# Pairing the value products of the third attention on TensorE, with a third pair of buffers for the turned probabilities

## The chip, the cores and the metric

The kernel runs on one core of one Trainium2 chip. The metric is the time of one execution on the device in microseconds (us), from three runs each. Beside these runs there is one profiled execution, from which all rows below are taken. It lasted 2522.84 us, and its span from the first to the last instruction is 2521.0 us.

## The reference, cut to what matters

Two transformer blocks follow each other on 512 tokens of width 1024. The first block has two layers with a differential attention. The second block has one layer with two attentions: a latent attention (MLA) and a sparse attention (NSA). The change touches only the last of these, which the code calls attention number 3 (`which > DEPTH`, with `DEPTH = 2`); the words "third attention" count kinds: differential, latent, sparse.

For eight heads of 64 columns in two key groups it computes three results, weighs each with a gate per token and head, and adds them:

```
p_c = softmax(where(valid_c, q kc^T * scale, NEG)) * valid_c    # 31 compressed keys
o_s = softmax(mask(q ks^T * scale)) vs                          # selected blocks, causal
o_w = softmax(mask(q kw^T * scale)) vw                          # window of 256, causal
o   = g0 * (p_c vc) + g1 * o_s + g2 * o_w
```

With 512 tokens all eight blocks of 64 keys are selected, so `o_s` is a plain causal attention over up to 512 keys.

## The kernel before, in words

Each engine runs its own straight program, written out in order, and waits on semaphores. Nothing is planned at run time: the order of the instructions in the code is the order on each engine.

**The steps.** `nsa_steps` (L304) lists 36 steps, numbered 0 to 35. Step 0 is a compressed step (kind "cmp") for the heads t and t + 4 of the first tile. Each of four tiles then has eight ordinary steps: for each block b of 128 queries one over the selected keys, which are (b + 1) times 128 wide, and one over the window, at most 384 wide. Behind block 1 of each tile but the last stands the compressed step of the next tile. So the compressed steps are 0, 5, 14 and 23. The tiles open at steps 1, 10, 19 and 28 and close at 9, 18, 27 and 35. The widest steps, with 512 keys, are 8, 17, 26 and 34. A step holds two heads, one on each half of the partitions.

**What a step asks of each engine.** TensorE computes the scores of both heads (`scores`, L2184, or L2179 in a compressed step). VectorE adds the masks and takes the maxima (`maxes`, L1319 and L1321; L1304 to L1307 if compressed). ScalarE takes the exponentials (L661). VectorE scales the first head's probabilities (`weigh`, L1355 to L1363, or L1335 to L1339 for both heads of a compressed step), ScalarE those of the second head (L684). TensorE transposes them into PSUM (`turn`, L2205, or L2201). ScalarE copies the result into SBUF (`copy`, L676). TensorE multiplies values by it and adds into one PSUM bank (`apply`, L2225; `apply` of a step that opens a tile also multiplies the compressed part, L2219). A compressed step has no `apply` of its own.

**TensorE's order.** `attention` (L2166) ends with a loop over s from 0 to 35; this text calls one pass "iteration s". In this attention an iteration holds `scores(s + 2)`, then `turn(s, 0)` and `turn(s, 1)`, then one or two pieces (three 512-column matmuls each, L2241) of another product, the gate projection `gate_nsa1`, and then `apply(s - 1)`. After the loop comes `apply(35)`.

**Who waits for whom.** `turn(s, 0)` waits for VectorE's `weigh(s)` and for the copy of `turn(s - 1, 0)`, whose PSUM bank it reuses. `apply` waits for the step's copy. The apply that opens a new tile also waits until the last tile's result has left its bank: ScalarE writes `y_hi` (L697) and VectorE `y_lo` (L1145). The loops of ScalarE (L693) and VectorE (L1379) have the same steps. VectorE does `maxes(s + 2)`, then `weigh(s + 1)` in its iteration s. ScalarE does `copy(s)`, the second half of `weigh(s + 1)`, then the exponentials of step s + 2. Both also split the next block of gate weights into a high part (ScalarE, L570) and a low part (VectorE, L1139), one at a time in this loop.

**Buffers.** The copied, turned probabilities lie in two pairs of buffers, the pair s % 2 for step s (`turned_to`, L389). `copy(s)` waits on the count `pv_done` that TensorE raises at the end of each `apply`, up to that of step s - 2.

Of the kernel before, what the change touches and what calls it, by code (L numbers as in the profile page):

```python
# [7 lines left out]
P = 128  # L8
# [3 lines left out]
DEPTH = 2  # L12
# [83 lines left out]
def program(nc, weights, ada, c_row_d, vecs_d, consts_d, x_t, p_t, pool_w, cmp_w1, cmp_w2, positions, out):  # L96
# [7 lines left out]
    with ctx:  # L104
        def sb(name, shape, dt=F32):
            return ctx.enter_context(nc.sbuf_tensor(name, shape, dt))
# [30 lines left out]
        pT = [sb(f"pT{i}", [P, S]) for i in range(2)]  # L137
        T = [sb(f"T{i}", [P, S]) for i in range(4)]
        qx = sb("qx", [P, 4, S])
# [34 lines left out]
        def sem(name):  # L174
            if name not in sems:
                sems[name] = ctx.enter_context(nc.semaphore(name))
            return sems[name]
# [73 lines left out]
        def evacuated(g, off4=0):  # L251
            return bank_free(g), TURN[g] + 1 + off4
# [47 lines left out]
        def turned_cmp(t, j):  # L300

            return (T[j] if t % 2 == 0 else qx[:, j, :])[0:CMP_W, :]
# [41 lines left out]
        def applied(which, s):  # L344

            done = [x for a in ATTENTION[:which] for x in a] + ATTENTION[which][:max(0, s + 1)]
            return sum(x["kind"] != "cmp" for x in done)
# [31 lines left out]
        def probs(which, m):  # L379

            return pads[:, m % 4, 0:S]

        def score_bank(m):
            return ps[2 + m % 4]
# [1 line left out]
        def both_scores(s):  # L386
            return psum[:, 2 + 2 * (s % 2):4 + 2 * (s % 2), :]

        def turned_to(s, j, diff):  # L389
            return pT[s % 2] if diff else (pT[0], pT[1], T[2], T[3])[2 * (s % 2) + j]  # L390

        def turns(which, s):

# [4 lines left out]
        def turn_bank(which, s, j):  # L398
            return ps[6] if which < DEPTH else ps[(6, 1)[(turns(which, s) + j) % 2]]
# [159 lines left out]
        def _(act):  # L559
            c = Counts()  # L560

            def split(n, g, off2=0, off4=0):

                if n >= NU:
                    return
                act.wait_ge(*loaded(n, off2))
                if n >= 2:
                    act.wait_ge(*tile_done(g - 1, off4))
                w = slice(0, width(n))
                act.activation(w_hi[n % 2][:, w], raw[n % 2][:, w], ACT.Copy).then_inc(sem("hi_made"), 1)  # L570
# [70 lines left out]
            def attention(which, between=None):  # L641
                steps = ATTENTION[which]
                diff = steps[0]["kind"] == "diff"
                along, plan = ALONG.get(which), pieces(which)
                n0, g0, _, tpu = ST[along[0]] if along else (0, 0, 0, 0)

                def exps(s):
                    x = steps[s]
                    for j in range(2):
                        exp(s, j, x)  # L650

                def exp(s, j, x):
                    m = 2 * s + j
                    if j == 0:
                        act.wait_ge(*c.next("max_made"))
                    if x["kind"] == "cmp":
                        act.activation(probs(which, m)[:, 0:P], score_bank(m)[:, 0:P], ACT.Exp)\
                            .then_inc(sem("exp_done"), 1)
                        return
                    k = m % 4  # L660
                    act.activation(probs(which, m)[:, 0:x["w"]], score_bank(m)[:, 0:x["w"]], ACT.Exp,  # L661
                                   bias=small[:, k:k + 1], scale=1.0,
                                   accum_out=small[:, 4 + k:5 + k]).then_inc(sem("exp_done"), 1)

                def copy(s, j, x):

                    act.wait_ge(*c.next("pT_in_psum"))
                    if applied(which, s - 2) > 0:

                        act.wait_ge(sem("pv_done"), applied(which, s - 2))  # L670
                    bk = turn_bank(which, s, j)
                    if x["kind"] == "cmp":
                        dst, src = turned_cmp(x["tile"], j), bk[0:CMP_W, :]
                    else:
                        dst, src = turned_to(s, j, diff)[:, 0:x["w"]], bk[:, 0:x["w"]]
                    act.activation(dst, src, ACT.Copy).then_inc(sem("pT_made"), 1)  # L676

                def weigh(s):

                    if "gate" not in steps[s]:  # L680
                        return
                    p = probs(which, 2 * s + 1)[:, 0:steps[s]["w"]]
                    act.wait_ge(*c.next("scale_made"))
                    act.activation(p, p, ACT.Copy, scale=small[:, 14 + s % 2:15 + s % 2])\  # L684
                        .then_inc(sem("second_weighed"), 1)

                exps(0)
                if between:
                    between(0)
                exps(1)  # L690
                if between:
                    between(1)
                for s in range(len(steps) + 2):  # L693
                    if s >= 2 and steps[s - 2]["closes"] and not diff:

                        act.wait_ge(sem("pv_done"), applied(which, s - 2))
                        act.activation(y_hi[:, steps[s - 2]["tile"], :], ps[7][:, :], ACT.Copy)\  # L697
                            .then_inc(sem("xhi_made"), 1)
                    if s < len(steps):
                        for j in range(1 if diff else 2):  # L700
                            copy(s, j, steps[s])
                        if s + 1 < len(steps):
                            weigh(s + 1)
                        if s + 2 < len(steps):
                            exps(s + 2)
                        for u, j, k in plan[s]:
                            if j == k == 0:
                                split(n0 + u + 1, g0 + u * tpu)
                            if k == KT - 1 and not diff:
                                to_gate(along[1] + tpu * u + j, g0 + tpu * u + j, 0, 0)  # L710
                    if diff and 1 <= s <= len(steps):
                        for u, j, k in plan[s - 1]:
                            if k == KT - 1:
                                to_gate_times(tpu * u + j, g0 + tpu * u + j)
# [1281 lines left out]
        def _(pe):  # L1996
# [169 lines left out]
            def attention(which, between=None):  # L2166
                steps, m0 = ATTENTION[which], MC[which]
                diff = steps[0]["kind"] == "diff"
# [39 lines left out]
                def apply(s):  # L2208
                    x = steps[s]
                    if x["kind"] == "cmp":  # L2210
                        return
                    pe.wait_ge(sem("pT_made"), TURNS[which] + turns(which, s + 1))
                    if diff and s == 0:
                        pe.wait_ge(*evacuated(ST[f"v{which}"][1] + 3))
                    if x["opens"] and any(y["closes"] for y in steps[:s]):
                        pe.wait_ge(*c.next("o_made" if diff else "x_made"))
                    for compressed in x.get("cmp", []):
                        pe.wait_ge(sem("vc_made"), 1)
                        pe.matmul(*compressed, start=True, stop=False)  # L2219
                    n = len(x["values"][0])  # L2220
                    for i in range(n):
                        for j in range(len(x["values"])):
                            v, p = x["values"][j][i], turned_to(s, j, diff)[:, i * P:(i + 1) * P]
                            a, b = (p, v) if diff else (v, p)
                            ins = pe.matmul(x["out"][j], a, b, start=x["first"] and i == 0,  # L2225
                                            stop=x["last"] and i == n - 1)
                    ins.then_inc(sem("pv_done"), 1)
# [22 lines left out]
                scores(1)  # L2250
                if between:
                    between(1)
                ahead = which > DEPTH
                for s in range(len(steps)):
                    if ahead and s + 2 < len(steps):
                        scores(s + 2)
                    for j in range(1 if diff else 2):
                        turn(s, j)
                    if not ahead and s + 2 < len(steps):
                        scores(s + 2)  # L2260
                    for at in plan[s]:
                        piece(*at)
                    if s >= 1:
                        apply(s - 1)
                apply(len(steps) - 1)

            def lam_sums():
                pe.wait_ge(sem("lam_terms"), 1)
# [139 lines left out]
            for k in range(KT):  # L2408
                w = weight(n, 56 * k, 56 * k + 56)
# [47 lines left out]
            for u in range(3):  # L2457
                ready(n + u)
                for i, t in enumerate((3, 2, 0, 1) if u == 0 else range(QB)):
# [4 lines left out]
                    for k in range(6):  # L2464
                        a, w = (f_hi[:, 2 + k, at], f_lo[:, 2 + k, at]), weight(n + u, 256 * k, 256 * k + 256)
# [292 lines left out]
```

## Time and profile before

| what | us |
|---|---|
| median of three runs | 2524.85 (2523.75 to 2526.11) |
| the profiled execution | 2522.84 |
| its span | 2521.0 |
| TensorE matmuls busy in the span | 2501.9 (99%) |
| VectorE busy | 1395.2 (55%) |
| ScalarE busy | 943.7 (37%) |
| the third attention, first loop scores to the next stage | 1970.84 to 2090.23 of the span |

A row of the time line has the start, the duration, the engine and line, the operation, the tile written and the tiles read, the shape and the number of instructions merged into the row. In brackets stands idle time of the engine before it and what ended it. PE is TensorE's matmuls, PEld its weight loads, DVE is VectorE and ACT is ScalarE. Matmuls are pipelined and their durations overlap, so the time that a group takes is read from its start to the start of the next group.

### The profile page before, as it was taken

The page shows a single profiled execution, that of the slowest core. Times are in us where ns is not written, and L with a number is a line of the kernel's source. Part 1 is how long each engine was busy: PE and PEld are TensorE (multiplying, and loading weights), DVE is VectorE, ACT ScalarE, POOL GpSimd, SP SyncE. Part 2 cuts the span into 40 slices and gives each one's busy share as a digit, 9 for nine tenths or more (in the row PEclk, how much of TensorE's full clock was granted, in tenths as well). Part 3 has the DMA queues.
Part 4 walks back from the last instruction along what each step waited for, and adds up shares of the span by engine and source line. Part 5 has one row for each costly group of instructions (what it writes and reads, how often), then busy time and mean ns, then how long its engine had stood idle before and what let it go on. Part 6 is the DMA issues. An engine that isn't in the chain of part 4 may idle for free.

```text
span 2521.0 us, 30069 instructions
## 1 busy us (share of the span) xinstructions
PE 2501.9 (99%) x11841; PEld 2023.9 (80%) x11841; DVE 1395.2 (55%) x1962; ACT 943.7 (37%) x1379; POOL 60.4 (2%) x77
## 2 busy tenths in 40 slices
PE   9999999999999999999999999999999999999999
PEld 7788888888888877888888888888777658888887
DVE  6556366645556655555663444566654676733433
ACT  5432334322334444223442232445544574422222
POOL 6000000000000000000001000000000001000000
PEclk9999999999999999999999999999999999999999
DMA  4222223444443311222343333222222111222222
GB/s 164 67 84 96 88 101 104 150 147 150 150 136 115 104 68 69 99 101 84 109 139 126 134 115 133 95 91 101 101 93 75 51 34 67 101 100 100 94 90 100
DMA packets 38629, 260.04 MB, mean 103 GB/s; under 512 B 4417, under 2 KB 4673, under 8 KB 8049
## 3 DMA queue, kind: packets, MB, share of 16 engines
q1 hardware_dynamic: 32976, 226.92, 26.2%
q10 hardware_dynamic: 5296, 30.20, 3.4%
q8 instruction: 83, 1.36, 0.2%
q0 software_dynamic: 240, 1.28, 0.2%
q14 instruction: 34, 0.27, 0.0%
HBM read 256.29 MB, written 2.10 MB: 102 GB/s over the span
## 4 chain that ended last, share of the span: by engine, by line
PE 94%; DVE 4%; ACT 1%; issue 1%; DMA 0%; SPq 0%; DVEq 0%; ACTq 0%
PE ps L2010 65%; PE ps L2037 9%; PE ps L2241 6%; PE ps L2063 5%; PE ps L2184 2%; PE ps L2225 2%; PE ps L2205 1%; PE ps L2467 1%; DVE w_lo L1139 1%; PE ps L2483 1%; PE ps L2163 0%; DVE a_lo L1263 0%; PE ps L2523 0%; PE ps L2329 0%; DVE T L1258 0%
## 5 line engine op out<-in xcount | busy, mean ns | idle before, releaser
L1139 DVE TENSOR_TENSOR w_lo<-raw,w_hi 128x2048 fp32r<-128x2048 f32 x208 | 477.5, 2295 | 325.1 <-ACT w_hi L570 275.3
L2010 PE MATMUL ps<-a_hi,w_hi 128*128 128x512 f32 x1408 | 550.4, 391 | 0.5 <-DVE w_lo L1139 0.3
L2010 PE MATMUL ps<-a_hi,w_lo 128*128 128x512 f32 x1408 | 547.9, 389 | 0.0
L2010 PE MATMUL ps<-a_lo,w_hi 128*128 128x512 f32 x1408 | 547.8, 389 | 0.0
L570 ACT ACTIVATE w_hi<-raw 128x2048 fp32r<-128x2048 f32 x198 | 376.4, 1901 | 404.0 <-PE ps L2010 338.2
L2010 PEld LDWEIGHTS ps<-a_hi,w_hi 128*128 128x128 f32 x1408 | 264.3, 188 | 57.2 <-issue 1.1
L2010 PEld LDWEIGHTS ps<-a_lo,w_hi 128*128 128x128 f32 x1408 | 264.4, 188 | 55.4 <-issue 1.0
L2010 PEld LDWEIGHTS ps<-a_hi,w_lo 128*128 128x128 f32 x1408 | 264.3, 188 | 54.8
L2010 PE MATMUL ps<-f_hi,w_hi 128*128 128x512 f32 x708 | 275.4, 389 | 0.0
L2010 PE MATMUL ps<-f_lo,w_hi 128*128 128x512 f32 x708 | 275.4, 389 | 0.0
L2010 PE MATMUL ps<-f_hi,w_lo 128*128 128x512 f32 x708 | 275.4, 389 | 0.0
L2010 PEld LDWEIGHTS ps<-f_hi,w_hi 128*128 128x128 f32 x708 | 132.9, 188 | 27.8
L2010 PEld LDWEIGHTS ps<-f_lo,w_hi 128*128 128x128 f32 x708 | 132.9, 188 | 27.5
L2010 PEld LDWEIGHTS ps<-f_hi,w_lo 128*128 128x128 f32 x708 | 132.9, 188 | 27.4
L878 ACT ACTIVATE T<-T 128x512 f32<-128x512 f32 x64 | 40.4, 632 | 213.8 <-DVE T L1678 213.8
L1705 DVE TENSOR_TENSOR h<-h,ps 128x512 f32<-128x512 f32 x64 | 43.9, 687 | 132.5 <-PE ps L2010 101.1
L661 ACT ACTIVATE pads<-ps,small 128x384 f32<-128x384 f32 (+3 forms) x160 | 81.9, 518 | 75.8 <-DVE small L1321 75.7
L2010 PE MATMUL ps<-y_hi,w_hi 128*128 128x512 f32 x272 | 106.9, 393 | 0.0
L2010 PE MATMUL ps<-y_hi,w_lo 128*128 128x512 f32 x272 | 105.9, 389 | 0.0
L2010 PE MATMUL ps<-y_lo,w_hi 128*128 128x512 f32 x272 | 105.8, 389 | 0.0
L2241 PE MATMUL ps<-a_hi,w_hi 128*128 128x512 f32 x224 | 98.1, 438 | 0.0
L2063 PE MATMUL ps<-w_hi,a_hi 128*128 128x512 f32 x240 | 97.0, 404 | 0.6 <-DVE pads L1894 0.4
(384 smaller groups left out, 3559.8 us busy)
## 6 DMA issues: line engine op xcount, KB each, us to landing
raw<-weights SPq DMA_DIRECT2D x209, 1024.0 KB, 4.9
ada_w<-ada ACTq DMA_DIRECT2D x24, 1024.0 KB, 4.9
merged<-cmp_w SPq DMA_DIRECT2D x2, 1024.0 KB, 5.8
out<-h SPq DMA_DIRECT2D x8, 256.0 KB, 2.0
h<-x_t SPq DMA_DIRECT2D x3, 512.0 KB, 7.1
raw<-weights SPq DMA_DIRECT2D x4, 256.0 KB, 5.1
kt<-c_row ACTq DMA_DIRECT2D x2, 512.0 KB, 3.6
pads<-p_t ACTq DMA_DIRECT2D x2, 512.0 KB, 4.0
```

The lines of the kernel that those rows point to most:

```text
L570: act.activation(w_hi[n % 2][:, w], raw[n % 2][:, w], ACT.Copy).then_inc(sem("hi_made"), 1)
L661: act.activation(probs(which, m)[:, 0:x["w"]], score_bank(m)[:, 0:x["w"]], ACT.Exp, bias=small[:, k:k + 1], scale=1.0, accum_out=small[:, ...
L878: act.activation(T[2 + t % 2][:, :], T[t % 2][:, :], ACT.Square).then_inc(sem("act_seq"), 1)
L1139: dve.tensor_tensor(w_lo[n % 2][:, w], raw[n % 2][:, w], w_hi[n % 2][:, w].bitcast(F32), ALU.subtract)\
L1705: dve.tensor_tensor(dst, dst, bank(g0 + 8 + t)[:, :].unsqueeze(1), ALU.add)\
L2010: ins = pe.matmul(dst, a[i], b[j], start=done == 0, stop=done == total - 1)
L2037: ins = pe.matmul(bank(g + j)[0:m, :], a[p], x[q][:, k0 + k, :], start=k == 0 and (p, q) == (0, 0), stop=k == kts - 1 and (p, q) == (1, 0))
L2063: ins = pe.matmul(bank(g)[:, :], a[i], w[j], start=half == k == i == j == 0, stop=half == 1 and k == 3 and i == 1)
L2184: ins = pe.matmul(score_bank(2 * s + j)[:, 0:x["w"]], q, k, start=True, stop=True)
L2205: ins = pe.transpose(bk[:, i * P:(i + 1) * P], p[:, i * P:(i + 1) * P], C("ident"))
L2225: ins = pe.matmul(x["out"][j], a, b, start=x["first"] and i == 0, stop=x["last"] and i == n - 1)
L2241: ins = pe.matmul(bank(g)[:, :], w[p], A[q][:, k, :], start=k == 0 and (p, q) == (0, 0), stop=k == KT - 1 and (p, q) == (1, 0))
```

## The change

`kept` gives the number of pairs of buffers: three in this attention, two in all others. The third pair is `qx[:, 2, :]` and `qx[:, 3, :]`. `copy(s)` now waits for the `apply` of step s - 3 here. On TensorE the steps whose values are due are gathered in the list `due`; they are issued when two are there. A compressed step adds nothing to the list.

```diff
-        def turned_to(s, j, diff):
-            return pT[s % 2] if diff else (pT[0], pT[1], T[2], T[3])[2 * (s % 2) + j]
+        def turned_to(which, s, j):
+
+            if which < DEPTH:
+                return pT[s % 2]
+            if which == DEPTH:
+                return (pT[0], pT[1], T[2], T[3])[2 * (s % 2) + j]
+            return (pT[0], pT[1], T[2], T[3], qx[:, 2, :], qx[:, 3, :])[2 * (s % 3) + j]
+
+        def kept(which):
+            return 3 if which > DEPTH else 2
...
-                    if applied(which, s - 2) > 0:
-
-                        act.wait_ge(sem("pv_done"), applied(which, s - 2))
+                    if applied(which, s - kept(which)) > 0:
+
+                        act.wait_ge(sem("pv_done"), applied(which, s - kept(which)))
...
-                ahead = which > DEPTH
+                ahead, due = which > DEPTH, []
                 for s in range(len(steps)):
                     if ahead and s + 2 < len(steps):
                         scores(s + 2)
...
                     for at in plan[s]:
                         piece(*at)
-                    if s >= 1:
-                        apply(s - 1)
-                apply(len(steps) - 1)
+                    if s >= 1 and steps[s - 1]["kind"] != "cmp":
+                        due.append(s - 1)
+                    if len(due) == 2 or due and (not ahead or steps[due[0]]["closes"]):
+                        for i in due:
+                            apply(i)
+                        due = []
+                for i in due + [len(steps) - 1]:
+                    apply(i)
```

In the other attentions `ahead` is false, and each step's values are issued in the same place as before. In this one the pairs are (1, 2) in iteration 3, (3, 4) in 5, (6, 7) in 8, (8, 9) in 10, (10, 11) in 12, (12, 13) in 14, (15, 16) in 17, (17, 18) in 19, (19, 20) in 21, (21, 22) in 23, (24, 25) in 26, (26, 27) in 28, (28, 29) in 30, (30, 31) in 32, (32, 33) in 34, and (34, 35) behind the loop, where these two already stood. The number and kind of all instructions is the same.

## Rows read from the trace of the kernel before

**Rows 1.** The page: chain that ended last, by engine.
```profile
PE 94%; DVE 4%; ACT 1%; issue 1%; DMA 0%; SPq 0%; DVEq 0%; ACTq 0%
```
**Rows 2.** Busy time by engine over the third attention: start:end, length, then engines.
```profile
1970.84:2090.23 119.39, 114.67 (x838) 73.62 (x837) 82.60 (x217) 86.34 (x251) 0.00 (x0) 1.00 0.11 36
```
**Rows 3.** Time line of TensorE, iterations 7 and 8.
```profile
1994.55 0.92 PE L2184 MATMUL ps<-kt,qt 64*128 64x384 f32 x4
...
1996.75 0.40 PE L2241 MATMUL ps<-a_hi,w_lo 128*128 128x512 f32 x1
1997.08 0.88 PE L2225 MATMUL ps<-pT,vt 128*64 128x128 f32 x12
1997.89 0.49 PE L2184 MATMUL ps<-kt,qt 64*128 64x128 f32 x4
1998.31 1.09 PE L2205 MATMUL ps<-consts_sb,pads 128*128 128x128 f32 x8
```
**Rows 4.** Time line of TensorE, end of the attention: values of steps 34 and 35.
```profile
2088.55 1.09 PE L2225 MATMUL ps<-pT,vt 128*64 128x128 f32 x16
2089.47 0.83 PE L2225 MATMUL ps<-T,vt 128*64 128x128 f32 x12
```
**Rows 5.** Time line of TensorE's weight loads, iteration 8 and the last pair.
```profile
2000.03 0.64 PEld L2225 LDWEIGHTS ps<-T,vt 128*64 128x64 f32 x12 [0.37 <-ACT pT L676]
...
2089.37 0.69 PEld L2225 LDWEIGHTS ps<-T,vt 128*64 128x64 f32 x12
```
**Rows 6.** Time line of VectorE: maxima of step 9, then weighing of step 8.
```profile
1995.51 0.90 DVE L1319 TENSOR_TENSOR ps<-ps,consts_sb 128x256 f32<-128x256 f32 x2
...
1997.59 0.54 DVE L1363 TENSOR_SCALAR pads<-pads,small,gt 128x512 f32<-128x512 f32 x1
```
**Rows 7.** Time line of TensorE, turns of steps 26 and 34.
```profile
2057.73 0.66 PE L2205 MATMUL ps<-consts_sb,pads 128*128 128x128 f32 x4 [0.90 <-ACT T L676]
...
2084.51 1.06 PE L2205 MATMUL ps<-consts_sb,pads 128*128 128x128 f32 x8 [0.50 <-DVE pads L1363]
```
**Rows 8.** Time line of TensorE, iteration 5: turn of compressed step 5.
```profile
1988.74 1.28 PE L2201 MATMUL ps<-consts_sb,pads 128*32 128x128 f32 x8
```
**Rows 9.** Time line of VectorE: step 5's second head weighed; low weights; step 15 weighed.
```profile
1988.99 0.29 DVE L1339 TENSOR_TENSOR pads<-pads,small 128x128 f32<-128x128 f32 x1
...
2017.95 2.28 DVE L1139 TENSOR_TENSOR w_lo<-raw,w_hi 128x2048 fp32r<-128x2048 f32 x1
...
2022.22 0.47 DVE L1363 TENSOR_SCALAR pads<-pads,small,gt 128x384 f32<-128x384 f32 x1
```
**Rows 10.** Time line of TensorE, iterations 11, 12, 14 and 15.
```profile
2009.05 0.39 PE L2241 MATMUL ps<-a_hi,w_lo 128*128 128x512 f32 x1
2009.61 1.07 PE L2219 MATMUL ps<-qx,kt 32*64 32x512 f32 x4 [0.17 <-issue]
2010.98 1.08 PE L2179 MATMUL ps<-kt,qt 64*128 64x32 f32 x16
2011.99 0.66 PE L2205 MATMUL ps<-consts_sb,pads 128*128 128x128 f32 x4
...
2020.08 0.66 PE L2225 MATMUL ps<-T,vt 128*64 128x128 f32 x8
2020.66 1.13 PE L2184 MATMUL ps<-kt,qt 64*128 64x512 f32 x4
2022.84 0.85 PE L2205 MATMUL ps<-consts_sb,pads 128*128 128x128 f32 x6 [1.04 <-DVE pads L1363]
```
**Rows 11.** Time line of VectorE, low part of tile 0, steps 12 and 30 weighed.
```profile
2008.82 0.68 DVE L1145 TENSOR_TENSOR y_lo<-ps,y_hi 128x512 fp32r<-128x512 f32 x1
2009.82 0.41 DVE L1363 TENSOR_SCALAR pads<-pads,small,gt 128x256 f32<-128x256 f32 x1
...
2069.85 0.41 DVE L1363 TENSOR_SCALAR pads<-pads,small,gt 128x256 f32<-128x256 f32 x1
```
**Rows 12.** Time line of ScalarE, before the turn of step 26.
```profile
2055.39 1.91 ACT L570 ACTIVATE w_hi<-raw 128x2048 fp32r<-128x2048 f32 x1
```

More of the change, by code:

```diff
@@ L674, in copy @@
                     else:
-                        dst, src = turned_to(s, j, diff)[:, 0:x["w"]], bk[:, 0:x["w"]]
+                        dst, src = turned_to(which, s, j)[:, 0:x["w"]], bk[:, 0:x["w"]]
                     act.activation(dst, src, ACT.Copy).then_inc(sem("pT_made"), 1)
@@ L2222, in apply @@
                         for j in range(len(x["values"])):
-                            v, p = x["values"][j][i], turned_to(s, j, diff)[:, i * P:(i + 1) * P]
+                            v, p = x["values"][j][i], turned_to(which, s, j)[:, i * P:(i + 1) * P]
                             a, b = (p, v) if diff else (v, p)
```

## The prediction

> **What bounds the kernel now.** I began with the chain that ended last. TensorE holds 94% of it, and VectorE 4% [rows 1]. So a change counts only if it shortens what TensorE does, or if it adds to or takes from the time that TensorE waits. The second view was the busy time of the stage. In its 119.39 us TensorE is busy for 114.67, VectorE for 82.60 and ScalarE for 86.34 [rows 2]. The rest, 4.7, is all of TensorE's pauses there. That is less than 0.2% of the kernel (5.05 us), which is about what a measurement of it can tell from no change. The third view was TensorE's time line, for the price of a group of value products. The last was the time line of VectorE and ScalarE beside it, for how long the result of each step had been ready when TensorE took it.
>
> **What is removed.** No instruction goes or comes. What goes is a change of group. Twelve value matmuls hold TensorE for 0.81 us, from 1997.08 to 1997.89 [rows 3]. Within a group a matmul takes (1.09 - 0.27) / 15 = 0.054, with 0.27 for the last one's own length [rows 4]. So the group is 12 x 0.054 = 0.65 and its end costs 0.16. Where two steps' values stand together already, sixteen matmuls take 2089.47 - 2088.55 = 0.92, of which 0.87 are the matmuls [rows 4]. The end costs 0.05 there. A join saves 0.11, and 15 of the 16 pairs are new: -1.65. The piece ahead of a group ends in the same 0.33 (1996.75 to 1997.08) whether values or scores follow, so nothing is gained there. From below, a join could save nothing; from above, the whole 0.16 (-2.4). I take the 0.11, which a joined pair shows.
>
> The weight loads say why. The load for a value group starts only with its first matmul, after 0.37 idle. In the joined pair it starts at 2089.37, 0.10 ahead of its matmul [rows 4, 5]. The Trainium skill, "TensorE: Matmul & The Clock Gate", Part 2, says that TensorE pulls weight loads ahead of running matmuls. If that held at every change of group, a join would save nothing and the sum below would be 1.65 higher. The 0.37 speaks against it here, and the sum goes by the rows.
>
> A second thing goes. The values of the steps 10, 19 and 28 open a tile and wait for `y_lo`, which VectorE ends at 2008.82 + 0.68 = 2009.50. TensorE's step from 2009.05 to 2009.61 is 0.56 instead of 0.33 [rows 3, 10, 11]. The change puts this group one iteration later, when `y_lo` is long done: three times 0.23, -0.69. These stalls can't give more.
>
> **What is moved.** The first step of each pair is applied one iteration later. That takes its matmuls from in front of the next turn, and they had hidden the work of VectorE. Step 8 shows it. Its turn needs VectorE to have done `maxes(9)` and then `weigh(8)`. `maxes(9)` begins 0.96 after the start of the scores of step 9 (1994.55, 1995.51), and `weigh(8)` ends at 1997.59 + 0.54 = 1998.13 [rows 3, 6]. Where TensorE plainly waits, at step 15, it starts at 2022.84, which is 0.15 behind the end of the weighing (2022.22 + 0.47 = 2022.69) [rows 9, 10]. So step 8 can be turned from 1998.28. It is turned at 1998.31: the slack is 0.03. The 0.81 of `apply(6)` stood in between. Without it TensorE arrives at 1997.50 and waits, and the 0.81 is done afterwards all the same. So the deferral costs 0.81 - 0.03 = 0.78.
>
> I went through the 15 deferrals in this way, in order, carrying the shift of each scores group on to the turns that depend on it:
>
> - Steps 17, 26 and 34 are like step 8, and their turns have no slack by the same two views: step 26 waits 0.90 for a copy that stands behind ScalarE's 1.91 split of weights, and step 34 waits 0.50 [rows 7, 12]. Each loses a cover of 0.81: 3 x 0.81 + 0.78 = +3.21.
> - Steps 5, 14 and 23 are compressed. The second head's turn waits for VectorE's long weighing: 1988.99 + 0.29 + 0.15 = 1989.43, inside a turn group that lasts 1.28 [rows 8, 9]. A cover of 0.58 (2020.08 to 2020.66 [rows 10]) goes in each: +1.74.
> - Behind step 14 stands the wait of 1.04 before step 15. It ends a run of VectorE that has the 2.28 split of weights in it [rows 9, 10]. The deferred 0.58, less the 0.11 of its join, falls into this wait and costs nothing: -0.48 with rounding.
> - Steps 12, 21 and 30 lose the largest cover: 2010.98 - 2009.61 = 1.37 each, the opening group. Step 12 is ready at 2009.82 + 0.41 + 0.15 = 2010.38 and turned at 2011.99, a slack of 1.61 [rows 10, 11]. The 1.37 go and so do the 0.23 of the `y_lo` stall, so 0.01 is left. Step 21 comes out at 0.04. Step 30 has no compressed scores ahead of it: it is ready at 2070.41, and falls short by 0.14 [rows 11]. Together +0.14.
> - Steps 3, 10, 19, 28 and 32 keep a slack of 0.76, 0.47, 0.45, 0.45 and 0.23. They cost nothing.
> - VectorE's first split of weights holds step 4's turn in both versions, so 0.04 of the first join is lost: +0.04.
>
> The third pair of buffers costs nothing. It lies in `qx`, in the same memory as the others. `copy(s)` waits for an `apply` that stands before `turn(s)` in TensorE's own order, so the turn that feeds the copy always ends that wait first, before and after.
>
> **The sum.** -1.65 - 0.69 + 3.21 + 1.74 - 0.48 + 0.14 + 0.04 = +2.3 us. The same shift holds for all that follows, since TensorE's chain runs on through the next stage. The profiled execution of 2522.84 would become 2525.1. The median of the runs is 2.0 above the profiled one, so I expect 2524.85 + 2.3 = 2527.2 us.
>
> **The rivals.**
>
> *The cover isn't missed.* The waits before the turns 8, 17, 26 and 34 don't grow, because VectorE gets its scores earlier as well. Then only the -1.65 and the -0.69 stand, and the pauses that a doubled group could cover (0.2 before step 13, 1.0 before step 15, about as much elsewhere) might shrink by up to 1.7. The time is -2.3 to -4.0, some 2521.7 us. For it: the total cover per two iterations is unchanged. Against it: the exposed step is the one behind the iteration without values, and step 8's chain starts with scores that this very iteration issues.
>
> *VectorE and ScalarE fall behind.* This is the one that ends slower by more than the bound. Its place is the turns of steps 12, 21 and 30, where I have a slack near zero. If their weighing comes d later than I worked out, for instance since ScalarE's copies and exponentials now crowd into a shorter iteration, then those three cost d each, step 32 costs d - 0.23 and steps 10, 19 and 28 cost d - 0.46. At d = 0.8 this is 2.4 + 0.57 + 1.0 = 4.0, so +6.3 and 2531.1 us. It passes 5.05 from about d = 0.63. For it: ScalarE is busy 86 of 119 us here [rows 2]. Against: it idles behind most copies of the narrow steps.
>
> *The join saves nothing.* The end of a group costs the same in the middle of a pair. Then +4.0 and 2528.8 us. For it: a semaphore wait still stands between the two steps. Against: the joined pair [rows 4].
>
> *The order doesn't change at all* can be left out: the list holds one step until the next is due.
>
> **How the numbers follow.** The forecast has 0.62 (its own range 2525.5 to 2529.0), the uncovered rival 0.15, the slow one 0.10, the join without a gain 0.11, anything else 0.02. The time is that of the forecast, 2527.2. The range goes down to 2521.8, which takes in most of the first rival, and up to 2530.6, at which the slow one begins; the runs' own spread of 1.2 either way is in it. Faster by over 5.05 would need more than all pauses of the stage: 0.03. Slower by over 5.05 is the slow rival and a tail: 0.10. Within: 0.87.
>
> **What would show it.** In the profile after, the rows of pairs should be 16 + 12 or 12 + 12 matmuls with 0.11 less than before. Ahead of the turns of steps 8 and 17 there should be an idle time of about 0.8 to 0.9 that was not there. The waits before the steps 26 and 34 should be near 1.7 and 1.3. The wait before step 15 should have shrunk to some 0.6, and the `y_lo` stalls should be gone. VectorE's and ScalarE's busy time should not change. I am wrong if the turns 8 and 17 start without a wait, if the steps 12, 21 or 30 wait by over 0.3, or if the stage comes out shorter than 119.4 us.

## The result: 2531.67 us after, 2524.35 before

The median of nine runs of the changed kernel is 2531.67 us (2527.46 to 2533.33), and that of nine runs of the kernel before is 2524.35 (2522.82 to 2526.11). The ratio is 1.0025, with a 95% interval from 1.0017 to 1.0033. So the kernel is slower by 7.3 us where I had forecast 2.3, and the time lies outside my range.

The profiled execution lasted 2527.46 us with a span of 2525.6, against 2521.0: 4.6 us more. The other 2.7 us is not in it. Each run comes with the mean clock granted to TensorE. The profiled run has 1.000, but the nine reach from 1.000 down to 0.997, and a run with a lower mean is longer. So there are two things to explain, and they are told apart below by "spans at a clock of 1.000" and by the mean over all runs.

**The stage.** The busy times over the third attention in the profile after:

```profile
1970.95:2094.88 123.93, 112.97 (x837) 73.91 (x836) 82.39 (x217) 86.55 (x251) 0.00 (x0) 1.00 0.11 35
```

The stage grew by 4.54, from 119.39 to 123.93 [rows 2], which is the whole of the span's growth but for rounding. VectorE and ScalarE did the same work. TensorE was busy for 1.7 less and its pauses grew from 4.7 to 11.0.

**The joins.** TensorE's time line, pair (6, 7) in iteration 8, with the columns as before:

```profile
2000.30 0.88 PE L2233 MATMUL ps<-pT,vt 128*64 128x128 f32 x12
2001.01 0.82 PE L2233 MATMUL ps<-T,vt 128*64 128x128 f32 x12
2001.76 0.49 PE L2192 MATMUL ps<-kt,qt 64*128 64x128 f32 x4
```

The pair takes 2001.76 - 2000.30 = 1.46. Alone, each takes 0.81 [rows 3]. This join saves 0.16, where I had taken 0.11. Read in the same way, the others save from 0.13 to 0.16, and the fifteen together 2.2.

**The covers.** The turns of the steps 8, 17, 26 and 34 in the same time line, the first with the scores ahead of it:

```profile
1997.50 0.49 PE L2192 MATMUL ps<-kt,qt 64*128 64x128 f32 x4
1998.61 1.06 PE L2213 MATMUL ps<-consts_sb,pads 128*128 128x128 f32 x8 [0.62 <-DVE pads L1371]
...
2029.58 1.06 PE L2213 MATMUL ps<-consts_sb,pads 128*128 128x128 f32 x8 [0.82 <-DVE pads L1371]
2060.52 0.65 PE L2213 MATMUL ps<-consts_sb,pads 128*128 128x128 f32 x4 [1.69 <-ACT T L684]
2088.55 1.06 PE L2213 MATMUL ps<-consts_sb,pads 128*128 128x128 f32 x8 [1.30 <-DVE pads L1371]
```

The first two waits are new, the others were 0.90 and 0.50 [rows 7]. By the starts of the groups, the turn of step 8 now comes 1.11 behind its scores (1997.50 to 1998.61) instead of 0.42 [rows 3], and the four together cost 3.1 us more than before. The bracket counts from the modelled end of the last matmul, so the starts are the safer measure.

**The compressed steps and step 15.** Turns of step 5 and step 15:

```profile
1988.32 0.60 PE L2209 MATMUL ps<-consts_sb,pads 128*32 128x128 f32 x4 [0.20 <-DVE pads L1347]
1989.38 0.60 PE L2209 MATMUL ps<-consts_sb,pads 128*32 128x128 f32 x4 [0.46 <-DVE pads L1347]
2024.38 0.84 PE L2213 MATMUL ps<-consts_sb,pads 128*128 128x128 f32 x6 [0.60 <-DVE pads L1371]
```

The turn of step 5, one row in [rows 8], is now split by a wait for each head. Steps 14 and 23 show the same. The three cost 2.4 more (0.65, 0.86 and 0.86 by the starts). The waits ahead of the steps 13 and 22, 0.3 each in the kernel before, are gone: -0.6. The wait ahead of step 15 shrank from 1.04 [rows 10] to 0.60.

**What I had not priced.** TensorE's turns of the steps 12, 19 and 30 and the first piece behind each:

```profile
2011.15 0.66 PE L2213 MATMUL ps<-consts_sb,pads 128*128 128x128 f32 x4
2012.74 0.47 PE L2249 MATMUL ps<-a_hi,w_hi 128*128 128x512 f32 x1 [0.94 <-ACT gate L729]
...
2035.30 0.44 PE L2213 MATMUL ps<-consts_sb,pads 128*128 128x128 f32 x2
2036.15 0.50 PE L2249 MATMUL ps<-a_hi,w_hi 128*128 128x512 f32 x1 [0.41 <-ACT gate L729]
...
2073.70 0.63 PE L2213 MATMUL ps<-consts_sb,pads 128*128 128x128 f32 x4
2075.22 0.50 PE L2249 MATMUL ps<-a_hi,w_hi 128*128 128x512 f32 x1 [0.89 <-ACT gate L729]
```

In the kernel before, the same pieces:

```profile
2012.40 0.48 PE L2241 MATMUL ps<-a_hi,w_hi 128*128 128x512 f32 x1
...
2034.12 0.44 PE L2205 MATMUL ps<-consts_sb,pads 128*128 128x128 f32 x2
2034.32 0.48 PE L2241 MATMUL ps<-a_hi,w_hi 128*128 128x512 f32 x1
...
2071.86 0.66 PE L2205 MATMUL ps<-consts_sb,pads 128*128 128x128 f32 x4
2072.27 0.48 PE L2241 MATMUL ps<-a_hi,w_hi 128*128 128x512 f32 x1
```

Each of these pieces is the first of a new gate tile. All gate tiles of this attention use one PSUM bank, so the piece waits until ScalarE has evicted the last one. From the turn at 2011.15 the piece would follow in 0.41, the pitch of these two groups in the kernel before (2011.99 [rows 10] to 2012.40); it follows in 1.59. The loss is 1.18, and by the same reading 0.65 and 1.11 at the other two: 2.9 in all. ScalarE's time line shows why the eviction is late:

```profile
2010.69 0.51 ACT L692 ACTIVATE pads<-pads,small 128x256 f32<-128x256 f32 x1 [1.49 <-DVE small L1365]
2011.11 0.46 ACT L669 ACTIVATE pads<-ps,small 128x256 f32<-128x256 f32 x1
...
2012.01 0.59 ACT L729 ACTIVATE gate<-ps 128x512 f32<-128x512 f32 x1
```

It stands behind the weighing of step 12, which waits for VectorE, and behind the exponentials of step 13, and it ends at 2012.01 + 0.59 = 2012.60, just ahead of the piece. In the kernel before, it ended 0.56 ahead of the piece at 2012.40:

```profile
2011.25 0.59 ACT L721 ACTIVATE gate<-ps 128x512 f32<-128x512 f32 x1
```

There `apply(10)` with its 1.37 stood between the last piece of the old tile and the first of the new one [rows 10], and hid the eviction. The change took it away.

**The sum of the stage**, read from the starts: joins -2.2, `y_lo` stalls -0.7, the four wide turns +3.1, the three compressed turns +2.4, step 15 -0.45, the waits ahead of the steps 13 and 22 -0.6, the turn of step 30 +0.1, gate bank +2.9. That makes +4.6, against a growth of 4.54. All other steps together come to nothing within 0.1.

### The profile page after: what moved, and what is told of

It is laid out like the page before. It is cut to its first block, busy times and chain, and to the rows that moved or that the text cites. A ratio compares the mean times of both kernels' runs of the same rounds, so it can differ in the third digit from the quotient of the medians.

```text
span 2525.6 us, 30069 instructions
## 1 busy us (share of the span) xinstructions
PE 2500.4 (99%) x11841; PEld 2024.0 (80%) x11841; DVE 1394.9 (55%) x1962; ACT 943.9 (37%) x1379; POOL 60.4 (2%) x77
## 4 chain that ended last, share of the span: by engine, by line
PE 93%; DVE 4%; ACT 1%; issue 1%; DMA 0%; SPq 0%; DVEq 0%; ACTq 0%
PE ps L2018 65%; PE ps L2045 9%; PE ps L2249 6%; PE ps L2071 5%; PE ps L2192 2%; PE ps L2233 2%; PE ps L2213 1%; PE ps L2480 1%; DVE w_lo L1147 1%; PE ps L2496 1%; PE ps L2171 0%; DVE ps L1327 0%; DVE a_lo L1271 0%; PE ps L2536 0%; PE ps L2342 0%
```

## The experiments

All kernels were timed in three groups, each beside the kernel before on one chip; the chips differ from group to group. A span at a clock of 1.000 is compared with those of the kernel before at 1.000: 27 of its 94 runs, 2520.8 to 2521.9, mean 2521.4 (2521.3, 2521.4 and 2521.4 on the three chips). Over all 94 the mean span is 2522.7, and 5 of them have a clock of 0.998 or less.

### The changed kernel again, twice (e1_again, e11_after_third)

No edit.

> The changed kernel once more, unedited. Its profiled execution was 4.6 us longer than that of the kernel before, at a TensorE clock of 1.000, but its nine runs had a median 7.3 us longer, with mean granted clocks from 0.997 to 1.000. Theory A (lost cover, gate wait and clock): the stage is again 4.5 us longer in the profile, of it 2.2 us of new waits for ScalarE's eviction of the gate product; runs whose clock is below 1.000 are longer by about 1.9 us for each 0.001, and if the profiled run is one of them, the lower clock lies in the third attention, behind its longest waits. Theory B (elsewhere): the stage is 4.5 us longer and the rest of the time, 2 to 3 us, is spread over other stages, or the lower clock lies in stages that the change doesn't touch.

> The changed kernel unedited, on the same chip as the fill and the covered version, as their control. Theory A: spans of 2525.3 to 2526.0 at a clock of 1.000, about half of the runs at 0.998 or less, mean span 2528 to 2529. Theory B (the earlier share of such runs was chance): as few as in the kernel before, 2 of 11 or fewer.

Medians 2529.33 and 2529.93 us, ratios 1.0019 (1.0010 to 1.0028) and 1.0024 (1.0015 to 1.0033). With the nine first runs there are 31. Four have a clock of 1.000 and spans of 2525.3 to 2526.3, mean 2525.8: +4.4 against the kernel before at 1.000. In 15 of the 31 the clock is 0.998 or less. The mean span is 2528.6, so +5.8 at all clocks: the clock's part is 1.4. The first nine runs alone, three of them at 0.997, have a mean span of 2528.9, only 0.3 above that. Their 7.3 compares medians, and the median of nine runs of such unequal length can fall well off their mean; that of all 31 is 2529.93, 5.6 above the median of the 94.

Both profiled runs were at 0.998. In the second, the stretches of 2 us around step 12 (length, then TensorE, its loads, VectorE, ScalarE, GpSimd, granted clock):

```profile
2010.00:2012.00 2.00, 1.68 (x21) 1.39 (x20) 1.58 (x7) 1.43 (x6) 0.00 (x0) 1.00 0.01 4
2012.00:2014.00 2.00, 1.39 (x7) 0.68 (x7) 1.53 (x7) 1.64 (x6) 0.00 (x0) 1.00 0.00 0
2014.00:2016.00 2.00, 2.00 (x14) 0.92 (x12) 0.00 (x0) 2.00 (x3) 0.00 (x0) 0.72 0.03 8
2016.00:2018.00 2.00, 2.00 (x9) 1.21 (x6) 1.06 (x2) 0.46 (x3) 0.00 (x0) 0.50 0.00 0
2018.00:2020.00 2.00, 2.00 (x11) 0.91 (x10) 1.79 (x8) 1.56 (x5) 0.00 (x0) 0.93 0.00 0
```

TensorE has worked on 32-column scores and transposes and then waited 0.94 for the gate bank, up to 2012.61. For 2.3 us more it works at full clock; from about 2014.9 to 2018.2 the clock is 0.50, the lower of its two levels (1.2 instead of 2.4 GHz). A second stretch of this kind lies behind the wait of step 26, at 2062 to 2066. The first of the two repeats has both as well. This is theory A; B had the loss elsewhere. The Trainium skill, "TensorE: Matmul & The Clock Gate", "HAM oscillation — how this bites in real kernels", says that pauses of TensorE between bursts of matmuls bring its clock down. Its example has longer pauses, so it bears on the direction alone; in these rows the clock falls 2.3 us behind the end of a pause of 0.94.

### The third pair of buffers alone (e2_buffers_only)

```diff
-                    if len(due) == 2 or due and (not ahead or steps[due[0]]["closes"]):
+                    if due:
```

> The third pair of buffers alone: each step's values are issued one step behind, as before. Theory A: no difference from the kernel before, within 1 us, and the stage at 119.4 us. Theory B (the buffers in qx or the later wait of the copies cost something): 1 us or more of the 7.3 us stays.

Median 2524.48 us, ratio 1.0002 (0.9993 to 1.0012), spans at 1.000 of 2521.1 and 2521.6. The buffers cost nothing. Its profiled run has one low stretch in this stage too (granted clock 0.62 from 2042 to 2044 and 0.53 from 2044 to 2046), behind the compressed scores of step 23, with no wait added: the stage can do this by itself. It is the only one of the five profiled executions of the kernel before and of the versions that add no wait (e2, e5, e9, e12) that has one in this stage. Of the seven of versions that add waits and fill none, five have one.

### The gate eviction moved (e3_gate_first, e9_gate_alone)

```diff
+                        for u, j, k in plan[s]:
+                            if k == KT - 1 and which > DEPTH:
+                                to_gate(along[1] + tpu * u + j, g0 + tpu * u + j, 0, 0)
                         if s + 2 < len(steps):
                             exps(s + 2)
...
-                            if k == KT - 1 and not diff:
+                            if k == KT - 1 and which == DEPTH:
```

The first has this edit in the changed kernel; the second has it with no step deferred.

> The changed kernel, with one thing moved on ScalarE: the eviction of a finished gate tile stands ahead of the exponentials of step s + 2 instead of behind them. Theory A: the waits of TensorE's pieces for the gate bank at steps 12, 19 and 30 (0.94, 0.41 and 0.89 us in the changed kernel) go down to 0.1 or 0.2 each, the stage gets 1.5 to 2.2 us shorter than the changed kernel's 123.9, and the median falls by 2 us or somewhat more. Rival (VectorE is the real limit behind those waits): the waits reappear before the next turns (steps 13, 20 and 31), and the stage stays within 0.5 us of 123.9.

> No step deferred, as in the kernel before; only ScalarE's eviction of the gate tiles stands ahead of the exponentials. Theory A: nothing waited for the gate bank in the kernel before, so nothing is gained: within 0.5 us of the kernel before at equal clock. Rival (the earlier eviction is a gain of its own, so that it explained the 2.3 us of the earlier run): 1 us or more faster.

In the changed kernel the median becomes 2527.85 us, ratio 1.0011 (1.0002 to 1.0020). The one run at 1.000 has 2523.0, 2.8 below the changed kernel's 2525.8. By the rows 2.5 of the 2.9 are gone. The piece of step 12 now follows its turn in 0.68, with no idle time shown, which is still 0.27 above the 0.41 of before; at step 30 0.20 are left and at step 19 nothing:

```profile
2012.45 0.66 PE L2216 MATMUL ps<-consts_sb,pads 128*128 128x128 f32 x4
2013.13 0.47 PE L2252 MATMUL ps<-a_hi,w_hi 128*128 128x512 f32 x1
```

With no step deferred the same edit gives 2524.19 us, ratio 0.9999 (0.9990 to 1.0008): it has nothing to gain there. So the waits for the gate bank came from the deferrals together with the place of the eviction, and VectorE was not the tie behind them.

### The deferrals split up (e7_exposed, e8_openers)

```diff
-                    if len(due) == 2 or due and (not ahead or steps[due[0]]["closes"]):
+                    if due and (not ahead or due[-1] not in (6, 15, 24, 32)):
```

The second has (10, 19, 28) in this place.

> The kernel with three pairs of buffers, and only the values of the steps 6, 15, 24 and 32 deferred by an iteration, which are those ahead of the turns of the 512-wide steps 8, 17, 26 and 34. Theory A: each of these turns waits 0.6 to 0.8 us longer, together +3.2, less 0.44 for four joins: +2.8 us at a clock of 1.000 (spans of 2523.6 to 2524.6), no wait for the gate bank, and the profile shows the four waits. Rival (the cost comes from the sum of all deferrals, not from these places): +0.5 us or less here.

> Only the values of the steps 10, 19 and 28, which open a tile, are deferred. Theory A (the gate bank is the new tie at steps 12 and 30): the y_lo waits go (-0.69), three joins save 0.33, step 30 loses about 0.1, and TensorE's pieces of steps 12 and 30 wait 0.9 us each for ScalarE's eviction: +0.9 us at a clock of 1.000, both waits to be seen. Rival (those waits came from the earlier deferrals, of steps 8 and 26, that had moved ScalarE's work): no wait for the gate bank, and 0.9 us faster than before.

The four deferrals ahead of the wide turns give a median of 2528.48 us, ratio 1.0015 (1.0006 to 1.0024). The run at 1.000 has 2524.1: +2.7, expected +2.8. This rests on one run. The wait of step 26 is that of the changed kernel, and behind it the clock falls in the profiled run (same columns as above):

```profile
2061.05 0.66 PE L2213 MATMUL ps<-consts_sb,pads 128*128 128x128 f32 x4 [1.69 <-ACT T L684]
```
```profile
2060.00:2062.00 2.00, 0.66 (x4) 0.42 (x4) 1.35 (x1) 2.00 (x5) 0.00 (x0) 1.00 0.00 0
2062.00:2064.00 2.00, 1.87 (x9) 1.21 (x11) 1.93 (x6) 2.00 (x6) 0.00 (x0) 0.72 0.00 0
2064.00:2066.00 2.00, 2.00 (x22) 2.00 (x22) 0.40 (x2) 1.35 (x6) 0.00 (x0) 0.50 0.83 262
```

The three openers give 2525.29 us, ratio 1.0008 (0.9999 to 1.0018). Five runs at 1.000 have 2522.4 to 2523.0, mean 2522.7: +1.3. The 0.9 that I expected took the brackets for the loss; with 1.18 and 1.11 it would have been +1.4, and with 0.16 for a join +1.2. The 0.94 ahead of the piece of step 12 is there without any earlier deferral. So taking `apply(10)` out of iteration 11 is enough for it. The waits ahead of the steps 13 and 22 are gone here too, and the turns of the compressed steps 14 and 23, ahead of which nothing is deferred, cost 0.27 and 0.26 more: those waits have moved there.

### Only the covered deferrals (e5_covered_gate_first, e12_covered_repeat, e13_covered_gate_last)

```diff
-                    if len(due) == 2 or due and (not ahead or steps[due[0]]["closes"]):
+                    if due and (not ahead or due[-1] not in (1, 8, 10, 17, 19, 26, 28, 30)):
```

The first two are one kernel, which has the moved gate eviction too. The third has the eviction in its old place.

> Only the eight deferrals that my ledger calls covered are kept (steps 1, 8, 10, 17, 19, 26, 28 and 30 are applied together with the next step); all other steps are applied alone, as before. ScalarE evicts the gate tiles ahead of the exponentials. Theory A (each deferral costs what it uncovers, and its join saves 0.11): eight joins -0.88, the three y_lo waits -0.69, two small remainders +0.2, so 1.4 us faster than the kernel before at equal clock: spans of about 2519.6 at a clock of 1.000, where the kernel before has 2520.8 to 2521.8. Rival (any deferral costs, whatever stands beside it): not faster than before, 2521 or more.

> The covered version again (eight deferrals, gate evicted first), since its gain is small. Theory A: spans at a clock of 1.000 of 2519.6 to 2520.6 against 2520.8 to 2521.8 of the kernel before, no or one run at 0.998 or less, median 1.2 to 2 us below the kernel before. Rival (the first result was the draw of the clock): the spans overlap and the median is within 0.5 us.

> The same eight deferrals, but with the eviction of the gate tiles where it was, behind the exponentials. Theory A: the waits for the gate bank at the steps 12, 19 and 30 come back (0.9, 0.4 and 0.9), so that the spans at a clock of 1.000 are about 2.2 us above those of the covered version with the eviction moved, some 2522. Rival (the place of the eviction matters only together with the exposed deferrals): within 0.5 us of that version.

The covered version has medians of 2522.20 and 2522.80 us. Its ratios are 0.9992 (0.9983 to 1.0001) and 0.9993 (0.9984 to 1.0002). Each interval alone just reaches 1. Its ten spans at 1.000 are 2519.6 to 2520.9, mean 2520.1, and the 27 of the kernel before are 2520.8 to 2521.9, so the two ranges overlap by 0.1 at one run: -1.3, expected -1.4. None of its 22 runs has a clock of 0.998 or less. It is the fastest of all kernels here. Its median is 1.8 to 2.0 below that of the kernel before, and its mean span over all runs 1.9, of which a third is the clock.

With the eviction in its old place the median is 2526.66 us, ratio 1.0005 (0.9996 to 1.0014), and the two spans at 1.000 are 2522.2 and 2522.8: 2.4 above the covered version. The wait ahead of step 12's piece is back, and the clock falls right behind it, at about 2013.2:

```profile
2013.02 0.58 PE L2249 MATMUL ps<-a_hi,w_hi 128*128 128x512 f32 x1 [0.92 <-ACT gate L729]
```
```profile
2012.00:2014.00 2.00, 1.08 (x4) 0.64 (x3) 1.83 (x8) 1.62 (x6) 0.00 (x0) 0.81 0.00 0
2014.00:2016.00 2.00, 2.00 (x6) 0.29 (x4) 0.10 (x1) 2.00 (x4) 0.00 (x0) 0.50 0.04 8
2016.00:2018.00 2.00, 2.00 (x12) 1.23 (x12) 0.00 (x0) 0.44 (x1) 0.00 (x0) 0.50 0.00 0
2018.00:2020.00 2.00, 2.00 (x9) 1.08 (x6) 0.92 (x2) 0.35 (x1) 0.00 (x0) 0.50 0.00 0
```

### The waits filled (e4_fill, e10_fill_small)

```diff
+                    if ahead:
+                        fill({8: 5, 17: 6, 26: 14, 34: 10}.get(s, 0))
                     for j in range(1 if diff else 2):
                         turn(s, j)
+                    if ahead and s in (12, 30):
+                        pe.wait_ge(sem("x_made"), c.n["x_made"] + 1)
+                        fill(7, True)
```

This is the second; `fill(n)` issues n products of a column of zeros with 128 columns of `qt` into the output bank. The first had 1, 1, 3 and 2 of them with 512 columns, and none at the steps 12 and 30.

> The changed kernel with seven more matmuls on TensorE, put into its longest waits: one ahead of the turns of steps 8 and 17, three ahead of step 26, two ahead of step 34. They multiply by a column of zeros and add nothing to the result. Each takes some 0.5 us, less than the wait it stands in. Theory A (the waits lower the clock): the stage stays at 123.9 us in the profile, but the clock is 1.000 in all or nearly all runs and the median comes down from 2531.7 to about 2527.5 us. Theory B (the clock has nothing to do with the waits): clocks and median as in the changed kernel, 2531 to 2532 us. Theory C (the waits are not really free): the stage gets longer by the 3.5 us of the matmuls, and the median with it.

> The changed kernel with small matmuls in its longest waits: 128-column products with a column of zeros, 5 ahead of the turn of step 8, 6 ahead of step 17, 14 ahead of step 26, 10 ahead of step 34, and 7 each ahead of the pieces of steps 12 and 30. One takes about 0.11 us, so that each group is no longer than its wait (the earlier fill had 512 columns, took 1.0 us for one and was longer than its waits). Nothing is added to the result. Theory A (an idle or thinly used TensorE in this stage lowers its clock in some executions, and the lower clock costs the part of the time that the waits themselves don't): spans at a clock of 1.000 stay at 2525.3 to 2526.0, while runs at 0.998 or less become rare (0 to 2 of 11 instead of about 5) and the mean span falls from 2528.5 to about 2526.8. Theory B (the clock does not depend on these waits): 5 of 11 or so at 0.998 or less, and the mean as in the changed kernel.

Both fills were longer than the waits, so neither is the clean test that I wanted. The first gave 2530.38 us, ratio 1.0022 (1.0013 to 1.0031), with spans at 1.000 of 2527.1 to 2527.4; a product of 512 columns takes 1.0 and not 0.5. The second gave 2533.55 us, ratio 1.0034 (1.0022 to 1.0047), with one span at 1.000 of 2530.4, since its seven products (two instructions each, so x14) take twice what I had reckoned:

```profile
2013.99 1.74 PE L2265 MATMUL ps<-qt,consts_sb 128*64 128x128 f32 x14
2015.66 0.50 PE L2249 MATMUL ps<-a_hi,w_hi 128*128 128x512 f32 x1
```

As to the clock, in the first its low stretch lies around step 12, where nothing had been filled, and 2 of 11 runs have 0.998 or less. In the second, with that wait filled too, it is 0 of 6, and its profiled run has no low stretch in this stage. That points to theory A, but does not show it: a stage that is 5 us longer differs in more than this, and six runs are few.

## Why the prediction was wrong

**What held.** TensorE as the only engine that counts; the buffers without a price; the covers of the steps 8, 17, 26 and 34 (+3.2 forecast, +3.1 read; with these four deferrals alone the span grew by 2.7, joins included, where 2.8 was expected); the end of the `y_lo` stalls; the part of the compressed steps and of step 15 in kind. The three compressed turns cost 2.4 instead of 1.74, but 0.5 of it are the waits of the steps 13 and 22, which moved there, as the version with the openers alone shows. The joins gave 2.2 instead of 1.65: I had priced the end of the first group and not the shorter second, though the last pair of before has that too (0.76 from 2089.47 [rows 4] to the next stage at 2090.23, not 0.81).

**The step that failed** is "I went through the 15 deferrals in this way". I asked of each deferral only whether the next *turn* would be late. But `apply(10)`, `apply(17)` and `apply(28)` stand also between the last piece of one gate tile and the first of the next, and that piece waits for ScalarE to free the bank. I left out this wait, though it stands in the code, since the trace of before has no idle time there. It is +2.9 us in the changed kernel. The moved eviction took 2.5 of it back by the rows and 2.8 by one run at equal clock, and the covered version with the eviction in its old place lost 2.4. With this term the forecast for the profiled execution would have been +5.2 by my sizes, and the span grew by 4.6. The upper end of my range was loose too: I let the slow rival begin at 2530.6, but 2524.85 + 5.05 is 2529.9.

My slow rival named the right engine, ScalarE, but the wrong consumers: it had the turns of the steps 12, 21 and 30 wait by up to 0.8. Step 30 waited 0.14 as forecast; the other two did not.

**The second miss** is the clock. No rival had it, though the changed kernel was to have waits of some 1.7 and 1.3 us by my own forecast. In the kernel before and in the versions that add no wait (e2, e9, e5, e12) the clock is at 0.998 or less in 6 of 136 runs. In those that add waits and fill none (the changed kernel, e3, e7, e8, e13) it is so in 31 of 75. In the five profiled runs of these that have a low stretch in this stage, each begins between 0.2 and 2.4 us behind the wait of step 12 or 26. So low clocks come with the added waits; that it is the waits themselves that bring them on is argued from the place and from the fills, and not shown. They are not the only cause, as the profiled run with the buffers alone shows. Which of the waits matters how much is open: e3, without the one at step 12, has 2 of 11, while e7, which has only those of the wide steps, has 5 of 11, and e8, which has only those for the gate bank, 4 of 11.

A part of the clock's draw has nothing to do with the change. At the start of the kernel TensorE waits 0.9 to 1.8 us for VectorE ahead of eight matmuls of one column. In 8 of the 14 profiled executions its clock then falls for some 3 us between 26 and 32 us, whatever the version; in the other six, the two of before and after among them, it does not. The one with the eviction alone moved (e9), with the columns as above:

```profile
26.00:28.00 2.00, 2.00 (x11) 1.66 (x12) 0.90 (x5) 1.30 (x3) 1.74 (x4) 0.75 0.04 8
28.00:30.00 2.00, 2.00 (x6) 1.61 (x5) 1.79 (x7) 1.25 (x2) 1.75 (x4) 0.50 0.00 0
```

The 7.3 us are thus 4.4 of longer stage at equal clock, 1.4 of clock as an average over 31 runs, and 1.5 of chance in the first nine, of which 0.3 are a lower clock on average and the rest is where their median fell.

## What to carry to other kernels

When work is moved off an in-order engine's path, list every wait that stands behind it up to its new place, also those that had no idle time in the trace; a bank that two tiles use one after the other is one of them. Moving work out of a gap gains only the cost of one change of group, here 0.13 to 0.16 us, while it exposes up to its whole length, here 0.6 to 1.4 us, wherever the next result was just in time; only the deferrals with slack are worth it. And where the best case of a change is a microsecond or two, compare runs at equal clock, for the clock moves the time by as much.

## What the runs showed of the hardware

Each of these products stands in the trace as two instructions. Where the products write the two halves of the output partitions in turn, as in a value group, an instruction takes (1.09 - 0.27) / 15 = 0.054 us [rows 4]. In the fill, which wrote always the same half with the same shape, it took (1.74 - 0.27) / 13 = 0.113. That points to the two heads' products overlapping; the fill differs in its operands too, which no run here tells apart. It would also explain why both fills took twice the time that I had expected of them. The Trainium skill, "TensorE: Matmul & The Clock Gate", Part 3, says that small matmuls placed in different column groups of the array run at the same time; the two figures agree with it.

TensorE's clock was at 0.50 for 3 to 7 us behind waits of 0.9 to 1.8 us that stand next to short matmuls, in a part of the executions, and in others of the same program not at all; once it was so without such a wait (e2).
